# A two-block transformer kernel on one core: the second MLP's down products by Strassen's scheme

## The reference, cut to what matters

```python
h2 = rmsnorm(x, norm_ffn)
x = x + (silu(h2 @ w_gate) * (h2 @ w_up)) @ w_down     # 1024 -> 2816 -> 1024
```

## Time and profile before

| | us |
|---|---|
| median of 3 runs (lowest to highest) | 1310.87 (1310.47 to 1311.3) |
| the profiled execution's own time | 1310.93 |
| its span | 1309.6 |
| TensorE busy | 1297.8 (99%) |
| VectorE busy | 789.7 (60%) |
| ScalarE busy | 672.8 (51%) |
| GpSimd busy | 749.5 (57%) |

### The profile page before, as it was taken

How to read it: one execution, slowest core, us unless ns; L and a number is a source line. 1 busy time by engine, 2 the same in 40 slices (tenths; PEclk the granted TensorE clock), 3 DMA queues, 4 the chain that set the end, 5 groups by cost and what they waited for, 6 DMA issues and landing times.

```text
span 1309.6 us, 20326 instructions
## 1 busy us (share of the span) xinstructions
PE 1297.8 (99%) x7923; PEld 1113.9 (85%) x7923; DVE 789.7 (60%) x1330; ACT 672.8 (51%) x1209; POOL 749.5 (57%) x486
## 2 busy tenths in 40 slices
PE   9999999999999999999999999999999999999999
PEld 6787778879898898988788787776789998899988
DVE  5796794966275462643468575756578761488621
ACT  4532585466463362544665547645576651366520
POOL 3643425977475565666467362634368774477752
DMA  9685245333333233323332112121123233233331
GB/s 378 238 312 206 80 152 193 113 113 113 97 106 113 88 106 113 97 97 98 128 112 82 49 53 78 50 65 38 60 81 114 97 114 97 97 99 112 97 125 52
DMA packets 41392, 150.95 MB, mean 115 GB/s; under 512 B 4304, under 2 KB 4816, under 8 KB 40528
## 3 DMA queue, kind: packets, MB, share of 16 engines
q1 hardware_dynamic: 40416, 146.36, 32.8%
q0 software_dynamic: 448, 2.62, 0.5%
q10 hardware_dynamic: 432, 0.67, 0.1%
HBM read 146.75 MB, written 2.10 MB: 114 GB/s over the span
## 4 chain that ended last, share of the span: by engine, by line
PE 85%; DVE 7%; ACT 3%; POOL 3%; issue 1%; DMA 1%; DVEq 0%; SPq 0%; ACTq 0%; POOLq 0%
PE bank L771 24%; PE bank L773 23%; PE bank L772 23%; PE bank L1284 2%; POOL wL L3506 2%; PE bank L818 1%; PE bank L820 1%; PE bank L819 1%; PE bank L872 1%; POOL acc L3516 1%; DVE small L2720 1%; PE bank L865 1%; PE bank L832 1%; PE bank L857 1%; DMA xq<-in_xt 1%
## 5 line engine op out<-in xcount | busy, mean ns | idle before, releaser
L3506 POOL TENSOR_TENSOR wL<-raw,wH 128x1024 fp32r<-128x1024 f32 x137 | 336.3, 2461 | 303.2 <-ACT wH L1652 300.0
L771 PE MATMUL bank<-hH,wH 128*128 128x512 f32 (+1 forms) x680 | 261.7, 385 | 1.6 <-POOL wL L3506 0.6
L773 PE MATMUL bank<-hH,wL 128*128 128x512 f32 (+1 forms) x680 | 251.8, 370 | 0.0
L772 PE MATMUL bank<-hL,wH 128*128 128x512 f32 (+1 forms) x680 | 251.6, 370 | 0.0
L1652 ACT ACTIVATE wH<-raw 128x1024 fp32r<-128x1024 f32 x137 | 143.7, 1050 | 162.3 <-PE bank L773 136.0
L771 PEld LDWEIGHTS bank<-hH,wH 128*128 128x128 f32 x680 | 128.4, 189 | 29.9 <-issue 6.5
L773 PEld LDWEIGHTS bank<-hH,wL 128*128 128x128 f32 x680 | 128.2, 189 | 22.8
L772 PEld LDWEIGHTS bank<-hL,wH 128*128 128x128 f32 x680 | 128.5, 189 | 20.2 <-issue 1.9
L771 PE MATMUL bank<-gH,wH 128*128 128x256 f32 x512 | 145.4, 284 | 0.3 <-POOL gL L3511 0.3
L773 PE MATMUL bank<-gH,wL 128*128 128x256 f32 x512 | 144.9, 283 | 0.0
L772 PE MATMUL bank<-gL,wH 128*128 128x256 f32 x512 | 144.9, 283 | 0.0
(11 more groups left out here) (485 smaller groups left out, 3087.3 us busy)
## 6 DMA issues: line engine op xcount, KB each, us to landing
raw<-in_wall SPq DMA_DIRECT2D x209, 512.0 KB, 3.4
rows<-in_wall SPq DMA_DIRECT2D x24, 1024.0 KB, 11.1
bra<-in_rpbw SPq DMA_DIRECT2D x8, 360.0 KB, 4.4
xq<-in_xt SPq DMA_DIRECT2D x2, 1024.0 KB, 6.9
xT<-in_xn SPq DMA_DIRECT2D x1, 2048.0 KB, 9.3
out_x<-xT SPq DMA_DIRECT2D x7, 256.0 KB, 2.1
vE<-in_ctxt SPq DMA_DIRECT2D x1, 1024.0 KB, 20.6
icn<-in_invc POOLq DMA_DIRECT2D x1, 1024.0 KB, 8.7
```

The costliest lines, as they stand in the source:

```text
L771: matmul(o, a_h, b_h, start=first, stop=False)
L772: matmul(o, a_h, b_l, start=False, stop=False)
L773: return matmul(o, a_l, b_h, start=False, stop=last)
L3506: tt(wL[i % NHL][:, 0:n], raw[load(c) % NRAW][:, 0:n], wH[i % NHL][:, 0:n].bitcast(F32), ALU.subtract).then_inc(s.w_lo, 1)
```

## The change

The down products are made by the same scheme of seven products. The 22 inner tiles are now taken in three groups of 8, 8 and 6; after each group's gate and up pairs come four down pairs (output tiles 2j and 2j+1), each over the group's four, four or three inner pairs. The scheme needs, for each inner pair (m even, m odd), four sums of the joined activations: `inner_sums` on VectorE, whose high parts ScalarE copies (`joined_sums`) and whose low parts GpSimd subtracts (`joined_sums_rest`), except in a group's last inner pair, where VectorE does it. The low part is written over the sum. In the first down pair of a group the last inner pair's part of all seven products is put off to the end (`FIRST_ORDER`). The up result is multiplied by rsx for every m. A chunk of a down pair in the group of 6 holds 6 blocks and 2 empty ones. The last output tile is joined and added in two halves. Output tiles finish in the order 1, 0, 3, 2, 5, 4, 7, 6.

```diff
-HALF = {"w_mlp_out": 8, "w_down_2": 11, "w_out_2": 4}
+HALF = {"w_mlp_out": 8, "w_out_2": 4}
+GROUPS = ((0, 8), (8, 16), (16, 22))
...
-    for half in range(2):
-        for m in range(11 * half, 11 * half + 11):
+    for lo, hi in GROUPS:
+        for m in range(lo, hi):
             for name, odd in (("w_up_2", 0), ("w_gate_2", 0), ("w_gate_2", 1), ("w_up_2", 1)):
                 tile(name, m, range(odd, 8, 2))
-        for m in range(8):
-            tile("w_down_2", m, range(11 * half, 11 * half + 11))
+        for j in range(4):
+            for i, odd in ((0, 0), (1, 0), (1, 1), (0, 1)):
+                tile("w_down_2", 2 * j + i, range(lo + odd, hi, 2))
+                plan.extend([None] * (4 - (hi - lo) // 2))
...
+SECOND = [pair for g, (lo, hi) in enumerate(GROUPS)
+          for pair in [("gate", m) for m in range(lo, hi)] + [("down", 4 * g + j) for j in range(4)]]
...
+    fH = at("fH", 16 * K, [128, 4, 1792], F32R)
+    fS = [at("fS", o, [128, 1024]) for o in places]
+    fSL = [at("fSL", o, [128, 1024], F32R) for o in places]
+    fA = [at("fA", o, [128, 256], F32R) for o in (R + 87 * K, R + 66 * K, R + 69 * K, R + 90 * K)]
+    fB = [at("fB", o, [128, 512], F32R) for o in (R + 88 * K, R + 67 * K, R + 70 * K, R + 72 * K)]
...
+        for n in range(G + 2, LAST_PAIR + 1):
+            deep = depth(n)
+            claimed = set()
+            for q in range(7):
+                j = sum_of(n, q)[0]
+                if j not in claimed:
+                    claim(BANK["sum", n, j])
+                    claimed.add(j)
+                if first_out(n):
+                    product_of(n, q, range(deep - 1), q in (0, 1, 4, 5), False)
+                else:
+                    product_of(n, q, range(deep), True, True).then_inc(s.prod, 1)
+            if first_out(n):
+                for q in FIRST_ORDER:
+                    mm = product_of(n, q, (deep - 1,), False, q in (2, 3, 4, 6))
+                    if q not in (5, 6):
+                        mm.then_inc(s.prod, 3 if q == 4 else 1)
+            sums_freed(n)
...
         def up_joined(m):
...
-            if m >= 11:
-                tt(u, u, rsx[:, :], ALU.mult).then_inc(s.x2_s, 1)
-                dve.wait_ge(s.x2_s, X2_S.up + m - 10)
+            tt(u, u, rsx[:, :], ALU.mult).then_inc(s.x2_s, 1)
+            dve.wait_ge(s.x2_s, X2_S.up + m + 1)
...
             tt(tm[2 + m % 2][:, :], u, tm[m % 2][:, :], ALU.mult).then_inc(s.gu, 1)
+            if m % 2:
+                inner_sums(m)
+
+        def inner_sums(m):
+            g = group_of(m)
+            i, done_ = (m - GROUPS[g][0]) // 2, ADD_V.fs + 4 * (m // 2)
+            x, y_ = tm[2], tm[3]
+            s1, s2, s3, s4 = (fS[i][:, 256 * n:256 * n + 256] for n in range(4))
+            if g:
+                dve.wait_ge(s.prod, group_freed(g - 1))
+            dve.wait_ge(s.gu, m + 1)
+            tt(s1, x[:, 256:512], y_[:, 256:512], ALU.add).then_inc(s.add_v, 1)
+            tt(s3, x[:, 0:256], x[:, 256:512], ALU.subtract).then_inc(s.add_v, 1)
+            dve.wait_ge(s.add_v, done_ + 1)
+            tt(s2, s1, x[:, 0:256], ALU.subtract).then_inc(s.add_v, 1)
+            dve.wait_ge(s.add_v, done_ + 3)
+            tt(s4, y_[:, 0:256], s2, ALU.subtract).then_inc(s.add_v, 1)
+            if m + 1 == GROUPS[g][1]:
+                dve.wait_ge(s.full, FULL.fs + m // 2 + 1)
+                dve.wait_ge(s.rest_v, REST.fs + m // 2)
+                rest(fSL[i][:, :], fS[i][:, :], fH[:, i, 768:1792], s.rest_v)
...
+        def down_odd(n):
+            m, b = 2 * (down_of(n) % 4) + 1, sum_bank(n, 1)
+            dve.wait_ge(s.sums, 5 * n + 4)
             tt(xT[:, m, :], xT[:, m, :], b, ALU.add).then_inc(s.x_out, 1)
...
+        def down_even(n):
+            m, b = 2 * (down_of(n) % 4), sum_bank(n, 3)
+            first_sum(n)
+            dve.wait_ge(s.sums, 5 * n + 5)
+            tt(xT[:, m, :], xT[:, m, :], b, ALU.add).then_inc(s.x_out, 1)
...
+        def last_even(n):
+            for i in range(2):
+                t = slice(256 * i, 256 * i + 256)
+                b = sum_bank(n, 3 + i)[:, t]
+                dve.wait_ge(s.prod, 7 * n + 6 + i)
+                dve.wait_ge(s.sums, 5 * n + 4)
+                tt(b, b, xu[n % 2][:, t], ALU.add).then_inc(s.sums, 1)
+                dve.wait_ge(s.sums, 5 * n + 5 + i)
+                tt(xT[:, 6, t], xT[:, 6, t], b, ALU.add).then_inc(s.x_out, 1)
...
+        for n in range(G, LAST_PAIR + 1):
+            if gate_of(n - 1) is not None:
+                up_joined(gate_of(n - 1))
+            elif n > G:
+                down_even(n - 1)
+            if G < n < LAST_PAIR:
+                weight_sums(n + 1)
+                piece_low(n + 1, 2)
+            if n > G:
+                product_sums(n)
+            if n < LAST_PAIR:
+                piece_low(n + 1, 4)
+            if gate_of(n) is not None:
+                gate_scaled(gate_of(n))
...
         def joined_rest(m):
+            i = (m - GROUPS[group_of(m)][0]) // 2
             pool.wait_ge(s.hi, HI.fb + m + 1)
-            rest(bl[m % 11], tm[2 + m % 2][:, :], bh[m % 11], s.rest_g)
+            if m % 2:
+                rest(fB[i][:, :], tm[3][:, :], fH[:, i, 256:768], s.rest_g)
+            else:
+                rest(fA[i][:, :], tm[2][:, 0:256], fH[:, i, 0:256], s.rest_g)
+
+        def joined_sums_rest(m):
+            i = (m - GROUPS[group_of(m)][0]) // 2
+            pool.wait_ge(s.full, FULL.fs + m // 2 + 1)
+            rest(fSL[i][:, :], fS[i][:, :], fH[:, i, 768:1792], s.rest_v)
```

More of the change, by code:

```diff
@@ L147, in paired, with group_of, pair_of, gate_of @@
 def paired(b):
-    return b[0] in ("w_gate_2", "w_up_2") or b[0] == "w_mlp_in" and b[2] >= 4
-def pair_of(name, m):
-    return (m - 4) // 2 if name == "w_mlp_in" else G + m
+    return b[0] in ("w_gate_2", "w_up_2", "w_down_2") or b[0] == "w_mlp_in" and b[2] >= 4
+def group_of(m):
+    return sum(m >= lo for lo, _ in GROUPS) - 1
+def pair_of(name, k, m):
+    if name == "w_mlp_in":
+        return (m - 4) // 2
+    return DOWN[4 * group_of(k) + m // 2] if name == "w_down_2" else GATE[m]
+def gate_of(n):
+    kind, m = SECOND[n - G] if n >= G else ("inner", None)
+    return m if kind == "gate" else None
+def down_of(n):
+    kind, d = SECOND[n - G] if n >= G else ("inner", None)
+    return d if kind == "down" else None
+def depth(n):
+    d = down_of(n)
+    if d is None:
+        return 4
+    lo, hi = GROUPS[d // 4]
+    return (hi - lo) // 2
+def first_out(n):
+    return down_of(n) is not None and down_of(n) % 4 == 0
+def group_freed(g):
+    return 7 * (DOWN[4 * g + 3] + 1)
 def high_of(n, q):
@@ L478, in _banks @@
     ring = itertools.cycle((2, 3, 4, 5, 6, 7))
-    for half in range(2):
-        of.update((("sum", G + 11 * half + m, j), next(ring)) for m in range(11) for j in range(4))
-        of.update((("w_down_2", 8 * half + m), next(ring)) for m in range(8 + half))
+    of.update((("sum", n, j), next(ring)) for n in range(G, LAST_PAIR + 1) for j in range(5 if n == LAST_PAIR else 4))
     return of
@@ L2480, in joined @@
                 act.wait_ge(s.product, done("w_out_2", 3, 7))
[L2481 to L2521, removed]
@@ new lines, in joined, with joined_sums @@
+            if m and m == GROUPS[g][0]:
+                act.wait_ge(s.prod, group_freed(g - 1))
+            if m % 2:
+                copy(fH[:, i, 256:768], tm[3][:, :], s.hi)
+            else:
+                copy(fH[:, i, 0:256], tm[2][:, 0:256], s.hi)
+        def joined_sums(m):
+            i = (m - GROUPS[group_of(m)][0]) // 2
+            act.wait_ge(s.add_v, ADD_V.fs + 4 * (m // 2) + 4)
+            copy(fH[:, i, 768:1792], fS[i][:, :], s.full)
+        for n in range(G, LAST_PAIR + 1):
+            m = gate_of(n - 1)
+            more = n < LAST_PAIR
+            if m is not None:
+                gate(m)
+            if first_out(n):
+                joined(m)
+                joined_sums(m)
+            if more:
+                piece_high(n + 1, 0)
+            if m is not None and not first_out(n):
+                joined(m)
+            if more:
+                piece_high(n + 1, 1)
+            if m is not None and m % 2 and not first_out(n):
+                joined_sums(m)
+            first_product(n)
+            if n == G:
+                for q in range(2, 7):
+                    piece_high(G + 1, q)
+                root_of("ffn", 32 * 1024, rsx, bank[7])
+                even_columns(G + 2)
+            elif more:
+                for q in range(2, 6):
+                    piece_high(n + 1, q)
+                if n + 1 < LAST_PAIR:
+                    even_columns(n + 2)
+                piece_high(n + 1, 6)
```

212 lines of the change are left out of this document (89 added, 123 removed).

## The result

The changed kernel takes 1318.8 us (median of six runs, 1314.75 to 1319.51) against 1310.93 before (six runs, 1310.42 to 1311.3): ratio 1.0054, 95% interval 1.0044 to 1.0064. It is slower by half a percent, clear of the noise. The forecast was 1316.5 in 1306 to 1321. The profiled execution took 1318.61 us with a span of 1317.1; its TensorE clock was granted at 0.997 in the mean. In the two runs at 1314.75 and 1315.81 it was 1.000, in the other four 0.996 or 0.997.

A forecast was written before the change was run, and what follows sets the result against it. The prediction took TensorE, busy 99% of the span, to bound the kernel. From 1310.93 us it took 9.30 for saved matmuls and added 13.2 for stops and 1.7 for the tail: 1316.5 us, range 1306 to 1321.

The forecast's parts named there:

- TensorE's stream, -9.30: Second MLP: 924 matmuls of 256 columns, 110.87 us, replace 120.17 us of down products; gain 9.30 us.
- 5.0 us more in each odd pair: VectorE's inner_sums: three of four sums wait for whole GpSimd instructions, so weight_sums starts 5.0 us later, 3.7 of it waiting.
- The lag of two pairs: VectorE's queue in the gate pairs: 5.0 us added, 3.36 caught up, so 1.64 us of lag per two pairs.
- The lag at the down pairs: VectorE's lag at each group's first down pair: 7.27, 5.28 and 2.84 us.
- The end part, 7.1 us: From a first down pair's start, lag aside, to the low part of its last sums: 7.1 us.
- The stops, 13.2 us: TensorE waits in the first down pairs for the last low sums: 5.7, 3.7 and 3.8 us, 13.2 in all.
- The tail, +1.7: Kernel's end: the last add ends 2.3 us behind TensorE instead of 0.62, adding 1.7 us (1.2 to 2).
- Edits at nothing: GpSimd's sums work, piece 0 after down pairs, chunk loads: about nothing; at depth 3, 0 to 1 us.
- no alternation: Rival at inner_sums: the four sums pass GpSimd without being held, the lag never grows; 1303.6 us, chance 0.12.
- One wait more or fewer: Rivals at inner_sums: fourth sum held too, 1326.6 us, chance 0.05; third sum not held, 1306.6 us, chance 0.15.

The follow-up runs named there:

- experiment 1: Changed kernel plus a GpSimd wait after each odd m until VectorE's four sums are done; 1304.31 us, ratio 0.9951 to the kernel before.
- experiment 3: Changed kernel plus GpSimd waits for VectorE's four sums after each odd m, except at a group's end; 1304.99 us.

## Why the prediction was right, and where a term was off

- **TensorE's stream, -9.30:** right at 0.120 us for each matmul, which the added ones take too. With the stops gone (experiment 1) the last matmul is at 1298.01 against 1307.10, 9.09 sooner; but 0.66 of that was there before the second MLP's stream began. Its second matmul, before and in experiment 1:

```profile
976.95 0.28 PE L772 MATMUL bank<-gL,wH 128*128 128x256 f32 x1
```

```profile
976.29 0.28 PE L825 MATMUL bank<-gL,wH 128*128 128x256 f32 x1
```

  From there to the last matmul are 330.15 and 321.72 us, 8.43 less. The other 0.9 are small delays of 0.1 to 0.3 in the first down pairs, which the sum had at nothing.
- **5.0 us more in each odd pair:** right in mechanism and size. The three held sums and the free fourth came in the order forecast. First sums lie 13.23 us apart behind an odd m (1009.58 to 1022.81) and 8.39 behind an even one (1001.19 to 1009.58); the prediction had 13.4 and 8.4. The lag of two pairs is thus 21.62 - 20.16 = 1.46 us, forecast 1.64.
- **The lag at the down pairs:** 7.27, 5.28 and 2.84 forecast, 3.9 (1052.79 against 1048.89), 3.9 (1177.00 against 1173.11) and 2.5 (1280.35 against 1277.84) measured. In groups 1 and 2 stops at product 2 had come before, 2.4 and 0.6 us from start to start, which the prediction allowed for as a shift; with the slow matmuls behind them they held TensorE back by 2.8 and 0.8, and by so much VectorE lagged less. The rest is the 1.46 in place of 1.64, three times or twice over.
- **The end part, 7.1 us:** from the first sum at 1177.00 to the end of fSL at 1184.06 are 7.06. Its 128x1024 subtraction took 1.23, forecast 1.22.
- **The stops, 13.2 us:** 10.9, so 2.3 too many. This is the term that was mis-sized: 1.4 of it is the lag of two pairs (0.18 too much, eight times), most of the rest is the delay behind earlier stops, of the next bullet.
- **The clock and the restarts:** both missing from the sum. The clock was granted lower behind two of the three long stops, 3.1 us, and the slow matmuls behind the nine stops cost another 0.9. From 977.10 (the same matmul as above) to the last one at 1312.91 are 335.81 us for 2674 starts, which at 0.120 would take 320.88: 14.9 more, and 10.9 + 3.1 + 0.9 is that. So the time came out above the forecast in four runs of six and below it in the two at full clock, where 1310.93 - 9.30 + 10.9 + 0.9 + 1.7 = 1315.1 lies beside the measured 1314.75 and 1315.81 (their stops were not traced; those of the profiled execution are taken). Errors of opposite sign, 2.3 too much and 4.0 left out, lie in the 2.3 us between 1316.5 and 1318.8: that the forecast came so near is in part luck.
- **The tail, +1.7:** the last add of the changed kernel,

```profile
1312.32 0.70 DVE L2950 TENSOR_TENSOR bank<-bank,acc 128x512 f32<-128x512 f32 x1
...
1314.91 0.42 DVE L3525 TENSOR_TENSOR xT<-xT,bank 128x256 f32<-128x256 f32 x1
```

  ends at 1315.33, 2.30 behind TensorE's 1312.91 + 0.12; before it was 0.62. That is 1.68, as forecast.
- **Edits at nothing:** held but for the small delays above. In experiment 1, which has all of them, no wait for a load, a bank or a piece stops TensorE, also at a depth of 3 (in the group of 6), and its time is within 1 us of the forecast for no alternation (1303.6).
- **Rivals:** the price of no alternation, 1303.6, is about what both ways of removing the alternation gave (1304.31 and 1304.14). One wait more or fewer did not occur. At a group's end GpSimd idled at first, so the first three sums were free (0.42) and the fourth, behind joined_rest, took 1.37 to 1.40: the order in the forecast's 7.1 us.

## What to carry to other kernels

Before short operations are given to VectorE, look at where their operands lie and at what GpSimd runs at that moment: with one operand in PSUM they cost 0.42 us each here, with both in SBUF 1.5 while GpSimd's queue was full. An engine with slack can be told to wait: 1.7 us of idling on GpSimd in every second pair was worth 14.5 us of the kernel. Count a stop of TensorE of 1.7 us or more, as here, as its length and a chance of some 1.5 us on top (2.9 in one run), and expect the time to scatter.

## What the runs showed of the hardware that was not expected

The granted clock fell behind single stops in a stream that was busy for hundreds of us before: not behind the stop of 1.1 us in experiment 3, in seven runs of nine behind 2.2, in eight of eleven behind 2.95 (by the mean clock of each run) and in all eleven behind 6.6. In the traces it was back at 1.00 some 3 to 6 us behind the stop. In a profiled execution the clock held behind 2.23 us, and it held in the changed kernel behind 1.65 in group 1 but not behind 1.66 in groups 2 and 3, so the length of the stop alone does not decide; what else does was not tested. And GpSimd's instruction pays for the alternation too: 1.47 and 1.48 us beside VectorE's sums against 1.30.
